# Slot sums moved behind the first block's gate products, in a two-layer attention and expert kernel on one core

## What is computed

```
g_idx  = argmax(h @ w_group)                       # 1 of 4 groups
top_v, top_i = top_k(e_logits of that group, 2)    # 2 of its 8 experts
gates  = softmax(g_logits)[g_idx] * softmax(top_v)
y[t]   = sum over the 2 experts e of token t:
         gate * ((silu(h[t] @ w_gate[e]) * (h[t] @ w_up[e])) @ w_down[e])
x      = x + g_f * y
```

## Time and profile before

| | us |
|---|---|
| median of 3 runs | 1778.39 (1777.6 to 1780.38) |
| the profiled execution | 1778.26 |
| its span, first to last instruction | 1776.4 |
| TensorE busy | 1635.4 (92% of the span) |
| VectorE busy | 657.1 (37%) |
| DMA | 523 MB, mean 295 GB/s |
| mean granted TensorE clock | 0.964 |

### The profile page before, as it was taken

One profiled execution on the slowest core, in us unless ns is written; L12 is line 12 of the kernel. 1 busy time (PEld: TensorE's weight loads), 2 busy tenths in 40 slices (PEclk: granted clock), 3 DMA queues, 4 the chain that ended last, 5 costly groups with the idle time before them and its releaser, 6 DMA issues.

```text
span 1776.4 us, 17703 instructions
## 1 busy us (share of the span) xinstructions
PE 1635.4 (92%) x6700; PEld 703.8 (40%) x6700; DVE 657.1 (37%) x1387; ACT 376.6 (21%) x920; POOL 71.2 (4%) x91
## 2 busy tenths in 40 slices
PE   5999998997999997998599999998898999979995
PEld 2445454452343332332244455444453333323331
DVE  2586565360323231223377222224531323213231
ACT  3224344231011010010220234333320101001000
POOL 1100001000000000000000000001100000000000
PEclk9999999998999998999699999998999999989998
DMA  9981724179999999999657122023399999999995
GB/s 353 371 309 39 272 95 182 59 270 418 427 426 372 427 427 427 427 428 405 245 190 233 52 68 75 0 101 140 122 368 428 426 423 426 428 427 427 428 426 214
DMA packets 104154, 523.14 MB, mean 295 GB/s; under 512 B 7622, under 2 KB 46007, under 8 KB 79486
## 3 DMA queue, kind: packets, MB, share of 16 engines
q1 hardware_dynamic: 78816, 485.18, 67.2%
q10 hardware_dynamic: 17262, 17.53, 3.0%
q0 software_dynamic: 7984, 19.20, 3.0%
HBM read 520.96 MB, written 6.37 MB: 297 GB/s over the span
## 4 chain that ended last, share of the span: by engine, by line
PE 81%; DMA 11%; DVE 4%; issue 1%; ACT 1%; SPq 1%; DVEq 0%
PE psum L2219 19%; PE psum L2250 11%; PE psum L2265 10%; PE psum L1968 9%; PE psum L1771 9%; PE psum L1940 4%; PE psum L1826 3%; DMA ring<-in_moe_w_up_dram 3%; DMA ring<-in_moe_w_down_dram 2%; DMA HT<-in_moe_w_up_dram 1%; PE psum L2197 1%; DMA XN<-in_moe_w_up_dram 1%; DMA HT<-in_moe_w_down_dram 1%; DMA XN<-in_moe_w_down_dram 1%; DMA ring<-in_ada_w_dram 1%
## 5 line engine op out<-in xcount | busy, mean ns | idle before, releaser
L2219 PE MATMUL psum<-ring,V 128*32 128x512 f32 (+2 forms) x1408 | 335.7, 618 | 32.0 <-DMA ring<-in_moe_w_up_dram 18.6
L2265 PE MATMUL psum<-V,W 128*128 128x512 f32 x448 | 221.3, 619 | 9.7 <-issue 4.5
L2250 PE MATMUL psum<-ring,V 128*32 128x512 f32 (+2 forms) x784 | 207.3, 612 | 22.0 <-DMA XN<-in_moe_w_down_dram 11.8
L1577 DVE TENSOR_TENSOR X<-X,psum 128x512 f32<-128x512 f32 x224 | 153.7, 687 | 122.2 <-PE psum L2265 121.8
L2219 PEld LDWEIGHTS psum<-ring,V 128*32 128x32 f32 (+2 forms) x1408 | 109.5, 132 | 203.5 <-issue 203.4
L1119 DVE SCALAR_TENSOR_TENSOR W<-ring,cact,W 128x512 f32<-128x512 f32 (+1 forms) x224 | 138.5, 618 | 7.7
L1010 ACT ACTIVATE V<-psum,modall,scls 128x128 f32<-128x128 f32 x216 | 81.3, 457 | 273.9 <-PE psum L2197 257.7
L2265 PEld LDWEIGHTS psum<-V,W 128*128 128x128 f32 x448 | 73.3, 190 | 156.5 <-DVE X L1577 86.1
L2219 PE MATMUL psum<-HT,V 128*32 128x512 f32 (+2 forms) x256 | 117.9, 615 | 9.7 <-DMA XN<-in_moe_w_up_dram 9.2
L2219 PE MATMUL psum<-XN,V 128*32 128x512 f32 (+2 forms) x272 | 123.6, 608 | 0.6 <-issue 0.3
L1019 ACT ACTIVATE V<-psum 128x512 f32<-128x512 f32 x28 | 16.7, 597 | 505.1 <-PE psum L2228 418.7
(11 more groups left out here) (326 smaller groups left out, 1789.0 us busy)
## 6 DMA issues: line engine op xcount, KB each, us to landing
ring<-in_moe_w_down_dram SPq DMA_DIRECT2D x49, 2048.0 KB, 23.0
ring<-in_moe_w_gate_dram SPq DMA_DIRECT2D x44, 2048.0 KB, 22.9
ring<-in_moe_w_up_dram SPq DMA_DIRECT2D x44, 2048.0 KB, 18.0
ring<-in_ada_w_dram SPq DMA_DIRECT2D x16, 2048.0 KB, 15.6
HT<-in_moe_w_gate_dram SPq DMA_DIRECT2D x10, 2048.0 KB, 19.6
XN<-in_moe_w_up_dram SPq DMA_DIRECT2D x9, 2048.0 KB, 20.9
XN<-in_moe_w_gate_dram SPq DMA_DIRECT2D x8, 2048.0 KB, 26.1
ring<-in_ada_w_dram ACTq DMA_DIRECT2D x16, 1024.0 KB, 5.3
```

Of the source, the lines that this page charges most:

```text
L1577: return dve.tensor_tensor(x3[:, c, cols], x3[:, c, cols], sum_bank(p, hf, c), ALU.add)
L2219: ins = pe.matmul(bank[2 + 2 * i + b][half * w:(half + 1) * w, :], V[:, col:col + w], slot3(x)[:, k, :], start=(k == 0), stop=(k == KC - 1))
L2250: ins = pe.matmul(bank[6 + hf][half * w:(half + 1) * w, :], HIDDEN_T[:, col:col + w], slot3(x, 4)[:, k, hf * HALF:(hf + 1) * HALF], start= ...
L2265: pe.matmul(sum_bank(p, hf, c), PICK[p % 2][:, c * P:(c + 1) * P], Y[:, hf * HALF:(hf + 1) * HALF], start=True, stop=True).then_inc(s["sum ...
```

## The change

The slot sums become a function of their own, `slot_sums`, which `gate_up` calls between the gate and the up products of block 0. The wait for `gate_row` (ScalarE has read banks 5 and 6), which stood ahead of the slot sums, now stands ahead of the rank product. The rank product writes bank 6 in place of bank 2, since gate products of block 0 write bank 2 and no longer stand behind the wait for `tab_f`. On VectorE the four copies of block 0's rows out of bank 3 stand ahead of the slot table.

```
                 dve.wait_ge(*s["rank_pe"](4))
-                step(dve.tensor_scalar(rank, bank[2][:, 64:64 + E], float(-FIXED), None, ALU.add))
+                step(dve.tensor_scalar(rank, bank[6][:, 64:64 + E], float(-FIXED), None, ALU.add))
...
-                step(dve.tensor_scalar(wide_base, bank[2][:, 64:64 + E], float(FIXED), float(FIXED + WIDE), ALU.max, ALU.min))
+                step(dve.tensor_scalar(wide_base, bank[6][:, 64:64 + E], float(FIXED), float(FIXED + WIDE), ALU.max, ALU.min))
...
-                dve.wait_ge(*s["tab_pe"](1))
-                slot_table(bank[6][:, 0:2 * NB], NB, slot_gate[:, :], None, tok[:, :], s["tok_ready"].sem, 912)
-                dve.wait_ge(*s["tok_ready"](1))
-
                 dve.wait_ge(*s["xr_pe"](2))
                 for q in range(4):
                     k = 4 + q
                     ins = dve.tensor_scalar(V[:, 2 * D + k * P:2 * D + (k + 1) * P], bank[3][:, q * P:(q + 1) * P],
                                             scl[:, 1, k:k + 1], mod[:, 24 + k:25 + k], ALU.mult, ALU.add)
                 ins.then_inc(s["ht2_v"].sem, 1)
+
+                dve.wait_ge(*s["tab_pe"](1))
+                slot_table(bank[6][:, 0:2 * NB], NB, slot_gate[:, :], None, tok[:, :], s["tok_ready"].sem, 912)
+                dve.wait_ge(*s["tok_ready"](1))
...
                 pe.wait_ge(*s["picked"](3))
-                pe.matmul(bank[2][:, 64:64 + E], ones[0:E, :], W[0:E, 816:816 + E], start=True, stop=True).then_inc(s["rank_pe"].sem, 1)
+                pe.wait_ge(*s["gate_row"](4))
+                pe.matmul(bank[6][:, 64:64 + E], ones[0:E, :], W[0:E, 816:816 + E], start=True, stop=True).then_inc(s["rank_pe"].sem, 1)
...
-                pe.wait_ge(*s["gate_row"](4))
-                ob = W[:, 432:432 + 4 * TC * NB].rearrange("p (a n) -> p a n", n=2 * NB)
-                pe.wait_ge(*s["tab_f"](1))
-                for a in range(2 * TC):
-                    ins = pe.matmul(bank[6][:, 0:2 * NB], W[:, 2048 + a * P:2048 + (a + 1) * P], ob[:, a, :],
-                                    start=(a == 0), stop=(a == 2 * TC - 1))
-                ins.then_inc(s["tab_pe"].sem, 1)
+                def slot_sums():
+
+                    ob = W[:, 432:432 + 4 * TC * NB].rearrange("p (a n) -> p a n", n=2 * NB)
+                    pe.wait_ge(*s["tab_f"](1))
+                    for a in range(2 * TC):
+                        ins = pe.matmul(bank[6][:, 0:2 * NB], W[:, 2048 + a * P:2048 + (a + 1) * P], ob[:, a, :],
+                                        start=(a == 0), stop=(a == 2 * TC - 1))
+                    ins.then_inc(s["tab_pe"].sem, 1)
...
                             hidden_t(between)
+                        if i and p == 0:
+                            slot_sums()
```

## The result

| | before | changed |
|---|---|---|
| median, us | 1778.88 (4 runs, 1777.60 to 1780.38) | 1790.37 (4 runs, 1788.28 to 1792.62) |
| the profiled execution, us | 1778.26 | 1788.28 |
| its span, us | 1776.4 | 1786.5 |

The ratio is 1.0069, with a 95% interval of 1.0055 to 1.0083: 11.5 us slower by the medians, where 5.2 were forecast.

The account below looks back on a forecast made before the run. The prediction took the stream of 2 MB weight loads to pace the expert stages, with TensorE releasing their slots. 1778.3 plus 5.2 (3.3 − 0.6 + 2.5) gave 1783.5 us; own range 1780.5 to 1786.5, whole range 1775.5 to 1788.0.

Parts of the forecast that it names:

- transposes late: Block 1's row transposes on TensorE wait for the later first gather: 5.9 us in layer 0, 5.0 in layer 1.
- slow clock behind the wait: Transposes and down products behind TensorE's new wait run at the slow clock: 2.0 us a layer, from 1.5 to 2.7.
- release of i12 (i13) late: Block 1 weight load into block 0's down-weight slots (i12 layer 0, i13 layer 1) released 7.9 and 7.0 us later.
- slack of the release: Delay a load into block 0's down-weight slots can take and still land at the same time: 4.3 and 4.2 us.
- the credit for the third gather: The late third gather fills some of each idle hole in the load stream: 0.3 us off per layer.
- The first gather now meets a full stream: Block 1's gather, issued later among weight loads, lands after 11.7 us in layer 0 and 10.8 in layer 1.
- The 0.6 us for a shorter wait ahead of the up products: Layer 0: block 1's up products run faster after a wait of 5.7 instead of 10.3 us: 0.6 us back.
- i8's lead and the gathers' bytes cancel: First load into block 0's gate-weight slots starts 1.9 us sooner, gathers' bytes take up to 2.5 back: 0 each layer.
- bank and order cost 0: Rank product in another bank and VectorE's row copies first delay nothing: 0 us, with 1.2 and 1.9 us to spare.
- (1): Rival: the two gathers hold each other up, the first landing after 16.3 us in layer 0; 1791.7 us, chance 0.12.
- (2): Rival: gathers land as fast as before, 7.1 and 8.2 us, and nothing is lost; 1778.3 us, chance 0.27.
- (3): Rival: gathers land fast, their bytes are free, and loads starting 1.87 us sooner gain each layer; 1774.6 us, chance 0.11.

Follow-up runs that it names:

- the kernels with 5 and 10 products: Kernel before with 5 or 10 products of ones, read by nobody, ahead of block 1's first transposes: 1780.22 us (ratio 1.0019) and 1787.81 us (1.0061).
- the halfway kernel: Changed kernel with the slot sums behind the eighth of block 0's 16 gate products: 1782.94 us, ratio 1.0030.
- the reordered one with held gathers: Kernel before, block 1's transposes behind block 0's down products, first two gathers held until block 0's gate products are done: 1782.21 us, ratio 1.0020.
- the reordered changed kernel: Changed kernel with block 1's transposes behind block 0's down products, block 2's between block 1's gate and up products: 1778.86 us, ratio 1.0004.
- the reordered one: Kernel before with block 1's transposes behind block 0's down products, block 2's between block 1's gate and up products: 1777.47 us, ratio 0.9995.

## Why the prediction was wrong

The direction and the mechanism held, at each step the profile names: the later gather, its landing in a full stream, TensorE's wait, the slow clock behind it, the late release of i12, the hole in the DMA, its way to the end. The sizes did not, and the time, 1790.37, came out above the whole stated range (1775.5 to 1788.0). In layer 0 (in layer 1 with the 4.25 us taken off that layer 0 had cost by then):

| term, us | forecast | profile |
|---|---|---|
| transposes late, layer 0 and 1 | 5.9, 5.0 | 5.7, 6.0 |
| slow clock behind the wait | 2.0, 2.0 | 3.4, 2.6 |
| release of i12 (i13) late | 7.9, 7.0 | 9.1, 8.5 |
| slack of the release | 4.3, 4.2 | 4.0, 4.1 |
| block 1's up products late | 3.3, 2.5 | 5.0, 4.4 |
| layer as a whole | 2.7, 2.5 | 4.3, 5.9 |

On this pair of profiles 4.9 us are missing from the forecast. The clock makes 1.9 of them, the later transposes 0.8 (all in layer 1), the credit for the third gather 0.6 and the slack 0.3; 1.5 us came in layer 1 behind block 1's up products, and in layer 0 the shorter wait gave back 0.2 more than forecast.

**The step that failed** is a mis-sized term, the largest of these: "I take 2.0" for the clock. With it right the forecast would have been 1785.4, still 5 us short. I had bounds of 1.5 to 2.7 us from the two long waits of before, and went below their middle since part of the stretch is waiting for ScalarE. It cost 3.4 in layer 0 and 2.6 in layer 1. Before, the up products had the slow clock for 5.6 us (from 434.45 to 440). Here it was at 0.50 from 410 to 420, and at 0.93 from 420 to 422: over all the transposes and the first half of the down products, 8.5 us behind the end of the wait. The bounds of 1.5 to 2.7 were taken from products that ran without a gap. Layer 1 came out inside them, layer 0 did not; that its small transposes and short waits for ScalarE kept the clock low for longer is my reading, and no run tests it. Keeping TensorE busy gave back 1.0069 − 1.0038, 5.5 us, about what the two terms make (6.0). Since all beyond the slack counts in full, an error of 1.4 us in such a term is an error of 1.4 us in the time, in each layer.

**The other terms.** "The first gather now meets a full stream" was right within 0.7 us in layer 0 and 0.5 in layer 1 (10.96 and 11.32 against 11.7 and 10.8). The slack of 4.3 was right within 0.8; the kernels with 5 and 10 products put it at 3.5 and 3.6. The 0.3 us that I took off for the third gather in the hole did not show. The 0.6 us for a shorter wait ahead of the up products was 0.4 (9.39 us against 9.80). That i8's lead and the gathers' bytes cancel, taken as 0 from bounds of 1.9 gained and 0.6 lost, is not contradicted, but not clearly shown either: where there is no lead the bytes cost 1.9 and 1.8 us of longer waits in the halfway kernel and 1.7 a layer in the reordered one with held gathers, and the reordered changed kernel, which has both, costs 1.4 in all by the medians (1778.86 − 1777.47), and its interval against the kernel before (0.9995 to 1.0014) includes no change, but overlaps a little with that of the reordered kernel with held gathers (1.0010 to 1.0029). That bank and order cost 0 held.

**What stays open.** The profile after is the fastest of four runs, and the median lies 2.1 us above it; where these 2 us are wasn't seen. In layer 1 the last load is 5.2 us late where block 1's up products were 4.4, and the 0.8 us between were not followed. The ends of the spans differ by 10.1 us where the last loads differ by 9.5; this sits in the last down products, which took 9.94 us in place of 9.19 with a longer stretch at 0.50 (about 5.8 us in place of 4.2). The kernel with 5 products has a span 2.0 us longer (1778.4), and 3.2 us by the medians; the second figure was not followed.

**The rivals.** (1) gave nearly the measured time by luck, by a mechanism that the kernel with the second gather held back excludes. (2) failed at the landing: 11 us, not 7. (3) failed with it, and the reordered changed kernel shows that without the wait there is no gain either.

No version beat the kernel before: the reordered one is level with it (0.9995, 0.9986 to 1.0004). It no longer waits for a late gather and loses only what its bytes take from the stream.

## What to carry to other kernels

Before moving work later, follow what it releases on the other engines: here 1.9 us of sums moved by 7 us took the gather behind it out of a pause in the DMA and into a full stream, where it needed 3 to 4 us more. A wait of TensorE costs its own length and the slow clock behind it; measured here 5 to 6 us and 2.6 to 3.4 us. And what is behind a gather in program order waits for it, needed or not: with the transposes behind the down products the same late gather cost nothing that shows where the loads were issued sooner as well, and 3.3 us where they were not.

## What the runs showed of the hardware

A gather of GpSimd, up to 128 rows of 4 KB, took 4.4 to 5.1 us to landing with the rings half empty (the halfway kernel), 7.1 to 9.6 us with loads in front that ran out meanwhile, and 10.7 to 12.1 us with two or more 2 MB loads queued; one issued 1.4 us behind another into such a stream took 15.6 to 16.4 us. A second gather behind it did not slow the first (11.1 against 11.0 us). A 2 MB load on idle rings landed after 8.1 to 8.7 us, in the stream every 4.9 us. After TensorE had been idle for 5.18 us, the granted clock was 0.50 (1.2 GHz) up to 420 in layer 0, though TensorE was at work again from 411.54.
